# Hybrid pool, convolution and attention block: the order of stores, loads and splits around the attention stage's gate projections

## The chip, the cores and the metric

The kernel runs on one core of a Trainium2 chip. The time is the device time of one execution in microseconds (us), with all inputs and outputs in the chip's memory (HBM). Lower is better. The engines are TensorE (PE in the rows), VectorE (DVE), ScalarE (ACT), GpSimd (POOL) and SyncE (SP, which here only starts transfers; its rows read SPq).

## What is computed

One layer for x of 4096 tokens by 1024 channels, in float32. The reference, cut to what matters here:

```
h = rms_norm(x, ln_g); proj = h @ w_in
u_pool, g_pool, c_a, c_b, g_conv, q, k, v, g_attn = split_columns(proj)
y_pool = pool_mixer(u_pool, pool_w, pool_scale)
y_conv = conv_module(c_a, c_b, conv_dw, conv_b, conv_ln_g, conv_ln_b, conv_pw)
y_attn = sliding_window_attention(q, k, v, attn_sinks)   # 8 query heads, 2 kv heads, window 128, ALiBi, sinks
y = concat([y_pool * silu(g_pool), y_conv * silu(g_conv), y_attn * silu(g_attn)])
x = x + y @ w_out
return rms_norm(x, final_g)
```

## The kernel before

Tokens are worked on in eight blocks of 512 (NB = 8, n from 0), each of four subtiles of 128 (j from 0). Each float32 product is made of three passes over a rounded part (hi) and the rest (lo): hi by hi, lo by hi and hi by lo. The program has three stages, one behind the other: attention for all eight blocks (0 to about 700 us of the trace), the pool and convolution branches for all blocks, and the output projection. The weights of the output projection are prepared during the attention stage.

Every engine has its own instruction list, in the order in which the code writes it, and semaphores join them. An engine that waits holds up all that stands behind it on its list; for SyncE that is every transfer that it has yet to start. Nothing reorders the lists.

**A block n of the attention stage, on each engine.**

- TensorE (`tensor.body`): `attend(n-1, 0)`, the projections q0 to q3 (during q3 it also sums the squares of the next x, `fold_sums`), then `attend(n-1, 1)`, v, and then the gate projections g0 to g3 with the scores of subtiles 1 to 3 put inside them (scores of subtile 0 stand between v and g0), and k of the next block. `attend(n-1, 1)` multiplies the probabilities of subtiles 2 and 3 with v. It waits until they are loaded and masked, and, since it writes the bank that the sum of squares was in, also until VectorE has taken that sum (`mean`, L282).
- ScalarE (`scalar.body`): hi parts of q, hi parts of the weight sums (`combos.split_hi`, L496), the squares of the next x, `st.scale` (L294; the next x times its reciprocal root, in four parts), the exponentials of the scores, the tanh of the gates, hi parts of the next x (L333).
- VectorE (`vector.body`): lo parts of q, `make_combos` (adds two pieces of the output weights, L488, waits for ScalarE's hi part, subtracts it, L500), `mean`, `output(n-1, 1)`, `next_x(part)` (turns a scaled part of x, L301), `take_scores` (L1039, L1043), `invert`, `gate_make`, and the turning of the probabilities in squares (L1068).
- GpSimd: scales the probabilities (L840), masks them after they are loaded (`mask`, L850), and takes the reciprocal root for x (`root`, L288).

**Probabilities** are turned by way of HBM: `store_probs` (L695, four transfers) writes a subtile to `p_scratch`, and `load_probs` (L702, L704) reads it back when the store has landed. Subtiles 2 and 3 of block n-1 are loaded at the start of block n.

**Weight sums.** `Combos` makes 28 sums or pieces of the output weights, five in each of the blocks 1 to 5 and three in block 6; those of a block have the slots 0 to 4. They pass through two stages of memory in turn (`stage[s % 2]`), so VectorE or ScalarE can begin with sum s only when the store of sum s - 2 has landed (`wait_free`). `combos.store` (L506) waits for the lo part, stores 512 KB, and after some sums starts loads of the next raw weights (L461). `store_xT` (L730) stores half of the block's split x, 2048 KB.

**The last block and the change of stages.** While the last block runs, SyncE and ScalarE load weight chunks of the next stage, and SyncE loads x in parts into `x_first` (L542). TensorE begins the next stage with the projections cb0 and ca0, and then runs `attend_last`, the product of subtiles 2 and 3 of block 7 with v. VectorE's list ends the attention with `gate_last`, and all of the next stage's VectorE work stands behind that. SyncE's list for the next stage begins with small constants (L1618 to L1621, taps and per-channel vectors, fetched element by element) and the weight chunk U, and then with `turn_loads`, the last transfers of probabilities.

## Time and profile before

| | |
|---|---|
| median of 3 runs | 1484.96 us (1483.4 to 1488.67) |
| the profiled execution | 1483.98 us |
| its span, first to last instruction | 1482.0 us |
| TensorE busy | 1368.3 us, 92% |
| VectorE busy | 1174.0 us, 79% |
| ScalarE busy | 548.4 us, 37% |
| GpSimd busy | 362.0 us, 24% |
| mean granted TensorE clock | 0.972 |

The profiled execution is 0.98 us under the median, and 1.98 us of it lie outside the span. From about 700 us on, TensorE is busy nearly without a break; its idle time lies before that.

### The profile page before, as it was taken

The page shows a single profiled execution, that of the slowest core. Times are in us where ns is not written, and L with a number is a line of the kernel's source. Part 1 is how long each engine was busy: PE and PEld are TensorE (multiplying, and loading weights), DVE is VectorE, ACT ScalarE, POOL GpSimd, SP SyncE. Part 2 cuts the span into 40 slices and gives each one's busy share as a digit, 9 for nine tenths or more (in the row PEclk, how much of TensorE's full clock was granted, in tenths as well). Part 3 has the DMA queues.
Part 4 walks back from the last instruction along what each step waited for, and adds up shares of the span by engine and source line. Part 5 has one row for each costly group of instructions (what it writes and reads, how often), then busy time and mean ns, then how long its engine had stood idle before and what let it go on. Part 6 is the DMA issues. An engine that isn't in the chain of part 4 may idle for free.

```text
span 1482.0 us, 20609 instructions
## 1 busy us (share of the span) xinstructions
PE 1368.3 (92%) x7070; PEld 1118.1 (75%) x7070; DVE 1174.0 (79%) x2381; ACT 548.4 (37%) x1421; POOL 362.0 (24%) x543
## 2 busy tenths in 40 slices
PE   6997979798897979894999999999999999999998
PEld 5876767676775767683888888888888888888886
DVE  5786859577685848470989999889899998888886
ACT  5744636464554536350211212212212243333332
POOL 4222313222221313140010110101101245555552
PEclk9999999899898999997999999999999999999999
DMA  9656482946556482858430321312326656455531
GB/s 215 208 140 262 117 297 91 277 151 193 204 142 249 107 276 72 256 204 165 157 122 21 128 101 56 127 55 101 128 72 241 273 167 226 160 164 156 163 138 73
DMA packets 117547, 239.18 MB, mean 161 GB/s; under 512 B 17488, under 2 KB 75216, under 8 KB 109776
## 3 DMA queue, kind: packets, MB, share of 16 engines
q1 hardware_dynamic: 93312, 214.24, 43.6%
q10 hardware_dynamic: 24144, 23.80, 6.6%
q8 instruction: 49, 0.80, 0.2%
q14 instruction: 42, 0.34, 0.1%
HBM read 139.44 MB, written 98.57 MB: 161 GB/s over the span
## 4 chain that ended last, share of the span: by engine, by line
PE 57%; DVE 19%; DMA 12%; SPq 5%; ACT 4%; issue 3%; POOL 1%; POOLq 0%; DVEq 0%; ACTq 0%
PE wide L346 12%; PE wide L347 12%; PE wide L348 12%; DMA p_scratch<-a_rows 6%; DVE a_rows L1043 4%; DMA combo_scratch<-stage 3%; DVE m_tail L2042 3%; PE turn L1232 3%; DVE xT L339 3%; DVE wide L1039 2%; PE pair L1265 2%; DVE a_rows L1068 2%; PE pair L1266 2%; PE pair L1271 2%; ACT a_rows L899 2%
## 5 line engine op out<-in xcount | busy, mean ns | idle before, releaser
L2042 DVE SCALAR_TENSOR_TENSOR m_tail<-m_tail,m_taps 128x512 f32<-128x512 f32 x480 | 338.5, 753 | 4.6
L1271 PE MATMUL pair<-xT,w_hi 128*128 128x512 f32 x384 | 154.2, 401 | 11.0 <-DVE xT L339 10.4
L840 POOL TENSOR_SCALAR a_rows<-a_rows,a_inv 128x128 f32<-128x128 f32 x256 | 94.3, 388 | 282.0 <-DVE a_inv L1063 223.7
L1265 PE MATMUL pair<-xT,w_hi 128*128 128x512 f32 x384 | 151.6, 395 | 3.5 <-DVE w_lo L410 3.5
L1266 PE MATMUL pair<-xT,w_lo 128*128 128x512 f32 x384 | 150.5, 392 | 0.0
L1784 POOL TENSOR_TENSOR operand_sums<-m_y 128x512 f32<-128x512 f32 x75 | 102.2, 1362 | 167.6 <-PE wide L348 116.6
L346 PE MATMUL wide<-x_first,w_hi 128*128 128x512 f32 x320 | 125.6, 392 | 1.5 <-DMA x_first<-xT_scratch 1.5
L346 PE MATMUL wide<-xT,w_hi 128*128 128x512 f32 x320 | 125.2, 391 | 0.0
L348 PE MATMUL wide<-x_first,w_hi 128*128 128x512 f32 x320 | 124.6, 389 | 0.0
L347 PE MATMUL wide<-x_first,w_lo 128*128 128x512 f32 x320 | 124.6, 389 | 0.0
L348 PE MATMUL wide<-xT,w_hi 128*128 128x512 f32 x320 | 124.5, 389 | 0.0
L347 PE MATMUL wide<-xT,w_lo 128*128 128x512 f32 x320 | 124.5, 389 | 0.0
L108 POOL TENSOR_TENSOR pool_carrier<-pool_carrier 128x1 f32<-128x1 f32 x23 | 14.1, 611 | 395.3 <-DVE m_meanvar L2051 395.3
L1871 ACT ACTIVATE x_first<-operand_sums 128x512 fp32r<-128x512 f32 x80 | 50.5, 634 | 153.7 <-POOL operand_sums L1784 152.4
L1271 PEld LDWEIGHTS pair<-xT,w_hi 128*128 128x128 f32 x384 | 72.2, 188 | 39.6 <-DVE xT L339 24.3
L1265 PE MATMUL wide<-xT,w_hi 128*128 128x512 f32 x256 | 101.3, 396 | 0.0
L1271 PE MATMUL wide<-xT,w_hi 128*128 128x512 f32 x256 | 99.8, 390 | 0.0
L1266 PE MATMUL wide<-xT,w_lo 128*128 128x512 f32 x256 | 99.7, 389 | 0.0
L899 ACT ACTIVATE a_rows<-a_rows,a_negmax 128x128 f32<-128x128 f32 x256 | 99.1, 390 | 0.0
L1232 PE MATMUL turn<-a_pT,a_v 128*64 128x128 f32 x256 | 24.6, 353 | 75.1 <-DVE a_meansq L282 50.6
L1265 PEld LDWEIGHTS pair<-xT,w_hi 128*128 128x128 f32 x384 | 72.5, 189 | 17.7 <-DVE w_lo L410 3.9
L1266 PEld LDWEIGHTS pair<-xT,w_lo 128*128 128x128 f32 x384 | 72.4, 189 | 13.9
(264 smaller groups left out, 3169.5 us busy)
## 6 DMA issues: line engine op xcount, KB each, us to landing
xT_scratch<-xT SPq DMA_DIRECT2D x16, 2048.0 KB, 11.8
p_scratch<-a_rows SPq DMA_DIRECT2D x128, 128.0 KB, 2.5
x_first<-xT_scratch SPq DMA_DIRECT2D x16, 1024.0 KB, 8.3
xT<-xT_scratch SPq DMA_DIRECT2D x16, 1024.0 KB, 9.2
combo_scratch<-stage SPq DMA_DIRECT2D x28, 512.0 KB, 7.3
m_y<-y_scratch ACTq DMA_DIRECT2D x14, 1024.0 KB, 6.6
xs<-in_x_dram SPq DMA_DIRECT2D x20, 512.0 KB, 9.8
a_pT<-p_scratch SPq DMA_DIRECT2D x16, 512.0 KB, 5.0
```

What stands on the lines that cost most here:

```text
L346: nc.tensor.matmul(out, w_hi, x_hi, start=first, stop=False)
L347: nc.tensor.matmul(out, w_lo, x_hi, start=False, stop=False)
L348: return nc.tensor.matmul(out, w_hi, x_lo, start=False, stop=last)
L840: last = nc.gpsimd.tensor_scalar(probs[b][:, h], probs[b][:, h], inv[:, b, h:h + 1], 0.5, ALU.mult, ALU.mult)
L899: last = nc.scalar.activation(probs[b][:, h], probs[b][:, h], ACT.Exp, bias=negmax[:, b, h:h + 1], accum_out=rowsum[:, b, h:h + 1])
L1043: last = nc.vector.tensor_tensor_reduce(out=probs[b][:, h], in0=in_runs(score[:, h, P:]), in1=in_runs(bias[:, h]), scale=1.0, scalar=sinks ...
L1232: return nc.tensor.matmul(out, weights[keys, halves[kv]], probs_of, start=start, stop=stop)
L1265: nc.tensor.matmul(out, w.hi(c)[:, kk, cols], st.hi[:, kk, :], start=(kk == 0), stop=False)
L1266: nc.tensor.matmul(out, w.lo(c)[:, kk, cols], st.hi[:, kk, :], start=False, stop=False)
L1271: last = nc.tensor.matmul(out, w.hi(c)[:, kk, cols], st.lo[:, kk, :], start=False, stop=(kk == KT - 1))
L1784: nc.gpsimd.tensor_tensor(operand_sums[:, i, 1], y_block(q, left), y_block(q, right), SIGN[op]).then_inc(operand_sum, 1)
L2042: nc.vector.scalar_tensor_tensor(out=conv[:, i, :], in0=h[:, i, j:j + TB], scalar=taps[:, i, j:j + 1], in1=conv[:, i, :], op0=ALU.mult, op ...
```

## The change

It has four parts. (A) In blocks 1 to 6 SyncE stores the first weight sum of the block (slot 0) before `load_probs(n-1, 3)` and no longer after it and after the first `store_xT`. The second sum is stored before the first `store_xT`, the third between the two. (B) ScalarE scales parts 0 and 1 of the next x ahead of the hi parts of the weight sums 3 and 4, part 2 ahead of the first exponentials and part 3 where part 2 was; VectorE turns parts 0 and 1 before it takes the first scores, part 2 where part 1 was and part 3 where part 2 was. (C) At the end of the attention stage SyncE stores subtile 2 before it waits for the chunk GP, loads it and stores subtile 3 before the next stage's list begins, and loads subtile 3 ahead of the small constants. (D) In the last block VectorE makes the lo part of chunk GP before it inverts the sums of subtile 3.

```diff
     def turn_loads(sp):
-        load_probs(sp, NB - 1, 2)
-        store_probs(sp, NB - 1, 3)
         load_probs(sp, NB - 1, 3)
...
                 load_probs(sp, n - 1, 2)
                 store_probs(sp, n - 1, 3)
+                for s in combos.of_block(n, (0,)):
+                    combos.store(sp, s)
                 load_probs(sp, n - 1, 3)
             st.wait_loaded(sp, n + 1)
...
+            for s in combos.of_block(n, (1,)):
+                combos.store(sp, s)
             store_xT(n, 0)
-            for s in combos.of_block(n, (0, 1)):
+            for s in combos.of_block(n, (2,)):
                 combos.store(sp, s)
             store_xT(n, 1)
-            for s in combos.of_block(n, (2, 3, 4)):
+            for s in combos.of_block(n, (3, 4)):
                 combos.store(sp, s)
...
+        store_probs(sp, NB - 1, 2)
         sp.wait_ge(w.lo_done[CHUNK_GP], 1)
         load_xT(sp, x_first, x_first_loaded, xT_scratch, 0, (2,))
-        store_probs(sp, NB - 1, 2)
+        load_probs(sp, NB - 1, 2)
+        store_probs(sp, NB - 1, 3)
...
             q_hi(n, 3)
+            if not final:
+                for part in (0, 1):
+                    st.scale(act, n + 1, part)
             for s in combos.of_block(n, (3, 4)):
                 combos.split_hi(act, s)
...
             if not final:
-                for part in (0, 1):
-                    st.scale(act, n + 1, part)
                 take_v()
+                st.scale(act, n + 1, 2)
                 for kv in range(KV):
                     exps(n, 0, kv)
                 act.wait_ge(st.squared_more, st.HALF * (n + 1))
                 gate_tanh(n, 0)
-                st.scale(act, n + 1, 2)
+                st.scale(act, n + 1, 3)
...
                 gate_tanh(n, 1)
-                st.scale(act, n + 1, 3)
...
             if not final:
-                next_x(0)
+                for part in (0, 1):
+                    next_x(part)
                 for kv in range(KV):
                     take_scores(n, 0, kv)
                 invert(SUB * n, 0, 0)
-                next_x(1)
+                next_x(2)
...
                 invert(SUB * n + 1, 1, 0)
-                next_x(2)
+                next_x(3)
                 invert(SUB * n + 1, 1, 1)
                 gate_make(n, 1)
-                next_x(3)
...
                     take_scores(n, j, 1)
+                    if j == 3:
+                        w.split_lo(dve, CHUNK_GP)
                     inverts(j)
...
                 step_of_v()
-                w.split_lo(dve, CHUNK_GP)
...
         sp.wait_ge(score_taken, ATTENDED)
+        w.load(sp, CHUNK_U)
+        attention.turn_loads(sp)
...
         sp.dma_start(pw[:], conv_pw[0].rearrange("(i p) d -> p i d", p=P)).then_inc(small_loaded, 16)
-        w.load(sp, CHUNK_U)
-        attention.turn_loads(sp)
         w.load(sp, CHUNK_GC)
```

SyncE's list in block 2, before, from the end of the store of subtile 3 (`p_scratch` is where the probabilities are turned, `combo_scratch` takes the weight sums, `raw` the pieces they are made of, `xT_scratch` the split x):

```order
L695 DMA p_scratch<-a_rows 32x4x256 x3
L702 DMA a_rows<-p_scratch 128x1024 [waits pv_full,a_probs_stored1]
L704 DMA a_rows<-p_scratch 64x512 x2
L730 DMA xT_scratch<-xT 128x4096 [waits x_loaded3,x_loaded2,xT_lo_done,x_loaded1,x_loaded0]
L506 DMA combo_scratch<-stage 128x2x512 [waits combo_lo] x2
L461 DMA raw<-in_w_out_dram 128x512 x2
L730 DMA xT_scratch<-xT 128x4096 [waits xT_lo_done]
L506 DMA combo_scratch<-stage 128x2x512 [waits combo_lo] x2
```

The same place in the changed kernel:

```order
L695 DMA p_scratch<-a_rows 32x4x256 x3
L506 DMA combo_scratch<-stage 128x2x512 [waits combo_lo]
L702 DMA a_rows<-p_scratch 128x1024 [waits pv_full,a_probs_stored1]
L704 DMA a_rows<-p_scratch 64x512 x2
L506 DMA combo_scratch<-stage 128x2x512 [waits x_loaded3,x_loaded2,combo_lo,x_loaded1,x_loaded0]
L461 DMA raw<-in_w_out_dram 128x512 x2
L728 DMA xT_scratch<-xT 128x4096 [waits xT_lo_done]
L506 DMA combo_scratch<-stage 128x2x512 [waits combo_lo]
L728 DMA xT_scratch<-xT 128x4096 [waits xT_lo_done]
```

The first sum's store now stands before the load of subtile 3, the second before the first store of split x, and the third behind that store instead of behind both.

SyncE's list at the change of stages, before (`x_first` is the first x of the next stage, `m_y` receives weight chunks, `in_w_in_dram` is the input projection):

```order
L542 DMA x_first<-xT_scratch 128x2048 [waits w_lo_done7]
L695 DMA p_scratch<-a_rows 32x4x256 [waits a_probs_loaded0,a_probs_squares_turned]
L695 DMA p_scratch<-a_rows 32x4x256 x3
L1618 DMA m_taps<-in_conv_dw_dram 128x31x1 [waits score_taken,score_full]
...
L1621 DMA m_pw<-in_conv_pw_dram 128x2x256
L390 DMA m_y<-in_w_in_dram 32x8x256 x4
L702 DMA a_pT<-p_scratch 128x1024 [waits pv_full,a_probs_stored0]
L704 DMA a_pT<-p_scratch 64x512 x2
L695 DMA p_scratch<-a_rows 32x4x256 [waits a_probs_loaded1,a_probs_squares_turned]
L695 DMA p_scratch<-a_rows 32x4x256 x3
L702 DMA a_rows<-p_scratch 128x1024 [waits pv_full,a_probs_stored1]
L704 DMA a_rows<-p_scratch 64x512 x2
```

The same place in the changed kernel:

```order
L695 DMA p_scratch<-a_rows 32x4x256 [waits a_probs_loaded0,a_probs_squares_turned]
L695 DMA p_scratch<-a_rows 32x4x256 x3
L542 DMA x_first<-xT_scratch 128x2048 [waits w_lo_done7]
L702 DMA a_pT<-p_scratch 128x1024 [waits pv_full,a_probs_stored0]
L704 DMA a_pT<-p_scratch 64x512 x2
L695 DMA p_scratch<-a_rows 32x4x256 [waits a_probs_loaded1,a_probs_squares_turned]
L695 DMA p_scratch<-a_rows 32x4x256 x3
L390 DMA m_y<-in_w_in_dram 32x8x256 [waits score_taken,score_full]
L390 DMA m_y<-in_w_in_dram 32x8x256 x3
L702 DMA a_rows<-p_scratch 128x1024 [waits pv_full,a_probs_stored1]
L704 DMA a_rows<-p_scratch 64x512 x2
L1626 DMA m_taps<-in_conv_dw_dram 128x31x1
```

The nine small transfers (L1618 to L1621, now L1626 to L1629) stood ahead of the load of subtile 2 and now stand behind the load of subtile 3.

## Rows read from the trace of the kernel before

**Rows 1.** Waits from 90 to 600 us: waiter <- releaser: us, times, longest.

```profile
PE turn L1232 <- DVE a_meansq L282: 50.6, 6, 11.1
...
DVE stage_sum L488 <- DMA combo_scratch<-stage: 32.5, 6, 6.9
...
ACT stage L496 <- DMA combo_scratch<-stage: 24.5, 4, 7.4
```

**Rows 2.** Timeline of SyncE in block 2: start, us, line, transfer, count.

```profile
187.96 2.00 SPq L695 DMA_DIRECT2D p_scratch<-a_rows  x4
195.53 0.34 SPq L702 DMA_DIRECT2D a_rows<-p_scratch  x1
...
197.18 0.45 SPq L730 DMA_DIRECT2D xT_scratch<-xT  x1
197.68 2.60 SPq L506 DMA_DIRECT2D combo_scratch<-stage  x2
200.32 2.58 SPq L461 DMA_DIRECT2D raw<-in_w_out_dram  x2
```

**Rows 3.** Timeline of VectorE in block 2; in brackets idle before and releaser.

```profile
199.91 1.39 DVE L1088 SCALAR_TENSOR_TENSOR a_q<-wide,a_q 64x512 fp32r<-64x512 f32 x2
206.32 0.69 DVE L488 TENSOR_TENSOR stage_sum<-raw 128x512 f32<-128x512 f32 x1 [5.02 <-DMA combo_scratch<-stage]
...
208.43 0.17 DVE L282 TENSOR_SCALAR a_meansq<-turn 128x16 f32<-128x16 f32 x1
...
218.40 0.69 DVE L500 TENSOR_TENSOR stage<-raw,stage 128x512 fp32r<-128x512 f32 x1 [6.25 <-ACT stage L496]
...
238.26 1.25 DVE L301 STREAM_TRANSPOSE xs<-xs 128x1024 f32<-128x1024 f32 x1 [0.92 <-ACT xs L294]
```

**Rows 4.** Timeline of ScalarE, then of GpSimd, in block 2.

```profile
217.73 0.63 ACT L496 ACTIVATE stage<-raw 128x512 fp32r<-128x512 f32 x1 [6.32 <-DMA combo_scratch<-stage]
218.27 3.30 ACT L294 ACTIVATE xs<-xs,a_rstd 128x256 f32<-128x256 f32 x8
...
200.09 1.29 POOL L850 TENSOR_TENSOR a_rows<-a_rows 128x512 f32<-128x512 f32 x1 [4.06 <-DMA a_rows<-p_scratch]
208.69 2.91 POOL L288 TENSOR_TENSOR a_rstd<-a_meansq,a_power 128x16 f32<-128x16 f32 x1 [7.31 <-DVE a_meansq L282]
```

**Rows 5.** Timeline of TensorE: first quarter of an attend, at 175 and 208 us.

```profile
175.41 1.09 PE L1232 MATMUL turn<-a_pT,a_v 128*64 128x128 f32 x16
...
208.66 1.97 PE L1232 MATMUL turn<-a_pT,a_v 128*64 128x128 f32 x16 [7.63 <-DVE a_meansq L282]
```

**Rows 6.** Windows: stretch, length, busy by engine, granted clock, DMA share, GB/s.

```profile
94.99:593.94 498.95, 434.14 (x2634) 346.81 (x2630) 349.13 (x999) 253.77 (x820) 119.04 (x222) 0.95 0.60 188
176.94:259.11 82.17, 72.21 (x443) 57.65 (x440) 58.34 (x169) 42.38 (x137) 19.89 (x37) 0.96 0.62 196
201.00:208.60 7.60, 0.03 (x1) 0.00 (x0) 1.85 (x4) 1.50 (x3) 0.38 (x1) 0.78 0.96 358
```

**Rows 7.** Timeline of SyncE at the change of stages.

```profile
666.30 2.45 SPq L695 DMA_DIRECT2D p_scratch<-a_rows  x4
...
681.03 0.40 SPq L702 DMA_DIRECT2D a_pT<-p_scratch  x1
...
682.70 1.96 SPq L695 DMA_DIRECT2D p_scratch<-a_rows  x4
690.53 0.34 SPq L702 DMA_DIRECT2D a_rows<-p_scratch  x1
```

**Rows 8.** Timeline of GpSimd and TensorE at the change of stages.

```profile
696.45 1.26 POOL L850 TENSOR_TENSOR a_rows<-a_rows 128x512 f32<-128x512 f32 x1 [5.66 <-DMA a_rows<-p_scratch]
...
666.51 0.62 PE L1232 MATMUL turn<-a_rows,a_pT 64*64 64x128 f32 x16
671.60 0.50 PE L346 MATMUL wide<-x_first,w_hi 128*128 128x512 f32 x1 [1.52 <-DMA x_first<-xT_scratch]
...
697.86 1.97 PE L1232 MATMUL turn<-a_pT,a_v 128*64 128x128 f32 x16 [17.80 <-POOL a_rows L850]
```

## The prediction

> **What bounds the kernel now.** I read the waits first, then the timelines of one block. Over the six blocks 1 to 6 of the attention stage TensorE stands still 50.6 us in six waits before `attend`, put down to VectorE's `mean` [rows 1]. In the same stretch VectorE waits 32.5 us and ScalarE 24.5 us for stores of weight sums to land. The reader is to see one chain in them, and the timelines of block 2 show it. SyncE issues the store of subtile 3 at 187.96, then stands until 195.53 for it to land before it can issue the load, and only after that, and after 2048 KB of split x, starts the store of the first weight sum, at 197.68 [rows 2]. VectorE is done with the lo part of q2 at 201.30 and then waits 5.02 us, to 206.32, because the third sum needs the memory of the first. So `mean` runs at 208.43 [rows 3] and TensorE, idle for 7.63 us, resumes at 208.66 [rows 5]. The first sum landed 8.6 us after its issue, right behind the 2048 KB. Within the wait the granted clock falls (0.78 over the idle stretch [rows 6]; between the levels 2.4 and 1.2 GHz that is full clock for some 4.3 of 7.6 us), and the first quarter of the attend takes 1.97 us, against 1.09 where TensorE came to it without a pause [rows 5].
>
> The fifth sum repeats this: it needs the third one's memory. The third was stored at 208.4, behind the second store of split x, and ScalarE's wait for it, 6.32 us, ends at 217.73 [rows 4]. VectorE's lo part follows at 218.40, and everything of the second half of the block stands behind it on VectorE's list. Block 2 takes 82.17 us and the six blocks 498.95 [rows 6].
>
> The second place is the change of stages. TensorE waits 17.80 us for GpSimd's mask of subtile 3 [rows 8]. Its load was issued at 690.53, its store at 682.70, and the load of subtile 2 before them at 681.03. The stretch from 668.75, the end of the store of subtile 2, to 681.03 is SyncE issuing nine small transfers and one weight chunk [rows 7]. After that TensorE has no gap of this kind.
>
> **Part A, the first sum's store.** No work is added; one 512 KB store is issued at 190.0 (187.96 + 2.00) instead of 197.68. Its lo part has been ready since before, so SyncE waits for nothing new. Even with the same 8.6 us it lands by 198.6, before VectorE wants the memory at 201.30. From there the sum's add, hi and lo take 0.69, 0.7 and 0.69 us, so `mean` runs at 203.4, 5.0 us earlier. TensorE's wait shrinks from 7.6 to 2.6 us, and its clock should stay full, since the fall came later than that.
>
> What is late next is the fifth sum. The third is stored at about 203.4: the second sum's store and two loads of raw weights are issued by 202.9 [rows 2], then comes the first store of split x, then the third sum. It again stands behind 2048 KB, so I take 8.0 us (row: 8.6, with a load of probabilities ahead as well that has by then been served; bounds 6.5 and 9.5). It lands at 211.4. ScalarE's hi part takes 0.63 us, VectorE's lo part starts at 212.1 instead of 218.40: 6.3 us earlier.
>
> Who waits for the store that is now ahead? The load of subtile 3. It is issued at the same 195.53 but has up to 512 KB more before it on the same queue, at the 358 GB/s of this stretch [rows 6] 1.5 us. GpSimd's mask then ends at about 202.9 instead of 201.38 [rows 4], still before 203.4. The bounds are 0 and 2 us; 2 would hold TensorE, not VectorE, which by my estimate is the later of the two by 1.4 us or more. The first store of split x is issued at 203 instead of 197.2; its memory is rewritten only near the end of the block, so that costs nothing.
>
> The Trainium skill, page "DMA: Bandwidth & Descriptors", section "Queues, rings and completion order", speaks against this edit: a queue's descriptors are taken in order on each engine, and the completion count is written only after all earlier writes of that engine, across queues. By that rule the load of subtile 3 cannot complete before the moved store, whatever its own size. The sum by it is the one above with 1.5 us on the mask, so nothing is lost in block 2, and up to 1.5 us where the mask comes last.
>
> **Part B, scaled x earlier.** The eight scalings take 3.30 us. They ran at 218.27, behind the hi part that waited for the store [rows 4]. Now they start when GpSimd's root is done: 203.6 + 2.91 = 206.5, ending at 209.8, inside ScalarE's wait. VectorE now turns two parts instead of one before the first scores, 1.25 us more there, and one fewer behind them. The last part's wait of 0.92 us [rows 3] goes too, because it is scaled one step earlier. So the first scores come 6.3 - 1.25 = 5.1 us earlier, and the end of the block 5.1 + 1.25 + 0.92 = 7.2 us earlier. Bound of the gain of part B alone: 0 to 2.2 us a block. In block 0 there are no sums; the turn ahead of the scores costs about 1.7 us there (half of the 3.30) and is given back behind. I take 0.
>
> **Sum of A and B.** Block 2 goes from 82.17 to 75.0 us. TensorE is busy 72.2 us in it [rows 6], of which nearly 2 us are the slow clock, so 75 is above its floor of about 70.5. The other blocks have the same work and their own lengths only from the same waits (the longest wait of the six is 11.1 us [rows 1]), so I take 75.0 for blocks 1 to 5, and 73.0 for block 6, which has no fourth and fifth sum. 5 x 75.0 + 73.0 = 448; 498.95 - 448 = 51 us gained. With the third sum landing in 9.5 instead of 8.0 us and 1.5 us more lost elsewhere it is 33; with 6.5 us TensorE becomes the limit after another 1.4 us a block, and it is 59.
>
> **Parts C and D.** D puts 2.3 us of VectorE work between the last scores and the inversion of their sums, in time in which ScalarE takes the exponentials; the subtile is turned about when it was. Priced 0, bound 1.5 us either way. For C, subtile 2 is stored before the chunk GP is waited for. Its load needs the memory that `attend(7, 0)` reads until 667.1 [rows 8]; it takes 1.67 us to issue (681.03 to 682.70 [rows 7]). The store of subtile 3 thus starts at 668.8 instead of 682.70, 13.9 us earlier. From that start to the end of its mask it took 15.0 us before (682.70 to 697.71): with the same delays the mask ends at 683.8. Before, one weight chunk and the load of subtile 2 lay unfinished ahead of the store; now the chunk lies behind it, ahead of the load. I take 2.8 us off: 681.0. TensorE gets there earlier too: x_first's part 2 is issued sooner, the 1.52 us wait [rows 8] goes, and its two projections end at 678.5. It waits 2.6 instead of 17.80 us and starts the attend 16.8 us earlier. At full clock the attend itself is shorter, by 0.9 us in its first quarter (1.97 against 1.09 [rows 5, 8]) and, by estimate, 2.6 us over all four. Together 19 us, bounds 12 (transfers as slow as before and a fallen clock) and 21. From there on TensorE is busy without a gap and the shift is kept to the end.
>
> **The sum.** 51 + 19 = 70 us off the profiled execution's 1483.98: 1414. The median is 0.98 above that execution, which makes 1415; I say **1414**, since the blocks 3 to 5 waited longer before than block 2.
>
> **Rivals.**
>
> 1. The second half gives part back: the third sum, behind 2048 KB, lands in 11 to 12 us, or x of the next block, whose loads share the queue with the moved store, comes later and holds VectorE before the second q. Then a block takes 78.5 to 79 us. For it: the DMA engines are busy 0.96 in this stretch [rows 6]. Against: the bytes are the same and a gap of 3 us opens. 5 x 78.7 + 76.5 = 470, 29 us gained; with 19: 1436.
> 2. The small constants come last. They are now issued from about 675 for 10 us and land near 688, while VectorE, after `attend_last` at about 684, wants the taps near 687. Against: TensorE needs what hangs on them only one projection later. If it bites, the change of stages gives 10: 1424.
> 3. Slower: the load of subtile 3 gets stuck behind the moved store in each block. It decides from the point where the mask ends after 208.5, that is, where the load lands more than 7 us later than now. If both took the place of the slowest rows of their kind, some 4 us a block would be lost after the gain is gone, 6 x 4 = 24, and with 19 - 0 kept at the change of stages the time is 1490. Only a wait of that size in every block does it, and 512 KB are 1.5 us.
> 4. The edit does not free the chain: the third sum waits for something else than the first one's store, such as raw weights or ScalarE. Then only the change of stages is won: 1465. Against: the wait of 5.02 us names the store [rows 3].
>
> **Chances.** Forecast 0.60 (its own range 1404 to 1428), rival 1 0.22, rival 2 0.10, rival 3 0.03, rival 4 0.05. The range must leave out no more than 0.2: 1402 to 1440 takes in the bounds of the sum and the rivals 1 and 2. Within 0.3%, 4.5 us, is about what a measurement of this kernel can tell from no change; only some of rival 3 lies there. Faster 0.96, same 0.02, slower 0.02.
>
> **What would show it.** In the profile after: first sum's store right behind the store of subtile 3; VectorE's wait for `combo_scratch` before `mean` gone; TensorE's six waits at `attend` 1 to 3 us each with the clock near 1.0; block length 73 to 76 us; the last mask at 680 to 684. Wrong would be: blocks of 78 us or more with ScalarE or VectorE waiting for the third sum (rival 1), VectorE idle before the taps after `gate_last` (rival 2), or GpSimd's mask as the last release of the attend with waits above 4 us (rival 3).

## The result, and the profile after

| | before | changed |
|---|---|---|
| median | 1484.83 us (1483.4 to 1488.67) | 1420.58 us (1418.57 to 1422.36) |
| ratio, 95% interval | | 0.9563 (0.9539 to 0.9587) |
| span of the profiled execution | 1482.0 us | 1417.2 us |
| six blocks, 1 to 6 | 498.95 us | 449.70 us |
| end of `attend(7, 0)` to end of `attend_last` | 36.3 us | 20.95 us |
| from there to the end | 778.6 us | 778.5 us |

The change saves 64 us. The spans differ by 64.8: 49.3 of them lie in the six blocks, 15.4 in the change of stages, and the rest of the program is only shifted. A block is taken, as in [rows 6], from the start of the third turning of squares (L1068, now L1073) to the next such start. The six are now 75.61, 76.90, 74.75, 72.20, 75.43 and 74.81 us.

The waits of the changed kernel from 85 to 560 us (waiter, releaser: us, times, longest), to be read against [rows 1]:

```profile
PE turn L1238 <- DVE a_meansq L282: 11.6, 5, 3.6
...
PE turn L1238 <- POOL a_rows L854: 2.7, 1, 2.7
...
DVE stage_sum L488 <- DMA combo_scratch<-stage: 17.9, 3, 7.0
...
ACT stage L496 <- DMA combo_scratch<-stage: 1.4, 1, 1.4
```

TensorE's 50.6 us before the second attend are 14.3. One of the six waits before, the longest (11.1 us, in block 5), did not go back to the landing of the first sum's store. There VectorE's idle time ahead of `mean` was for raw weights:

```profile
458.25 0.69 DVE L488 TENSOR_TENSOR stage_sum<-raw 128x512 f32<-128x512 f32 x1 [8.64 <-DMA raw<-in_w_out_dram]
```

Their load stands right behind the store of the first sum on SyncE's list, so the same order held it back. Block 2, SyncE, the stretch of [rows 2] (start, us, line, transfer, count):

```profile
181.20 1.99 SPq L695 DMA_DIRECT2D p_scratch<-a_rows  x4
...
183.24 0.47 SPq L506 DMA_DIRECT2D combo_scratch<-stage  x1
188.96 0.34 SPq L702 DMA_DIRECT2D a_rows<-p_scratch  x1
...
194.88 0.46 SPq L728 DMA_DIRECT2D xT_scratch<-xT  x1
197.49 0.38 SPq L506 DMA_DIRECT2D combo_scratch<-stage  x1
```

The first sum leaves 5.7 us ahead of the load of subtile 3, not 2.2 us behind it. VectorE in the same block, to be read against [rows 3] (in brackets idle before and releaser):

```profile
194.41 1.66 DVE L488 TENSOR_TENSOR stage_sum<-raw 128x512 f32<-128x512 f32 x1
196.77 0.69 DVE L500 TENSOR_TENSOR stage<-stage_sum,stage 128x512 fp32r<-128x512 f32 x1 [0.70 <-ACT stage L496]
197.49 0.17 DVE L282 TENSOR_SCALAR a_meansq<-turn 128x16 f32<-128x16 f32 x1
...
206.56 0.69 DVE L500 TENSOR_TENSOR stage<-raw,stage 128x512 fp32r<-128x512 f32 x1 [1.33 <-ACT stage L496]
```

The third sum's add comes without a wait, and the lo part of the fifth sum runs 36.2 us behind the block's start, before 41.5. TensorE, the second attend in three of the six blocks, and the windows of the six blocks (length, busy by engine, granted clock, DMA share, GB/s), against [rows 5] and [rows 6]:

```profile
120.60 1.09 PE L1238 MATMUL turn<-a_pT,a_v 128*64 128x128 f32 x16 [1.50 <-DVE a_meansq L282]
197.72 1.97 PE L1238 MATMUL turn<-a_pT,a_v 128*64 128x128 f32 x16 [3.60 <-DVE a_meansq L282]
273.89 1.09 PE L1238 MATMUL turn<-a_pT,a_v 128*64 128x128 f32 x16 [2.75 <-POOL a_rows L854]
...
94.80:544.50 449.70, 427.52 (x2633) 341.98 (x2630) 349.64 (x998) 253.12 (x820) 119.30 (x222) 0.98 0.67 209
```

The other three waited 1.65, 2.92 and 1.96 us. Of a block's 75 us TensorE is now busy 71.3. In block 7, which the change leaves as it was, TensorE waits 6.77 us for the mask at the same place in both kernels:

```profile
574.75 1.98 PE L1238 MATMUL turn<-a_pT,a_v 128*64 128x128 f32 x16 [6.77 <-POOL a_rows L854]
```

The change of stages, SyncE, then GpSimd, TensorE and VectorE, against [rows 7] and [rows 8]:

```profile
619.43 2.30 SPq L695 DMA_DIRECT2D p_scratch<-a_rows  x4
621.83 2.33 SPq L390 DMA_DIRECT2D m_y<-in_w_in_dram  x4
624.88 0.34 SPq L702 DMA_DIRECT2D a_rows<-p_scratch  x1
...
626.39 0.59 SPq L1626 DMA_DIRECT2D m_taps<-in_conv_dw_dram  x1
627.02 5.52 SPq L1628 DMA_DIRECT2D m_conv_bias<-in_conv_b_dram  x1
632.59 0.48 SPq L1628 DMA_DIRECT2D m_ln_gain<-in_conv_ln_g_dram  x1
...
632.92 1.26 POOL L854 TENSOR_TENSOR a_rows<-a_rows 128x512 f32<-128x512 f32 x1 [9.27 <-DMA a_rows<-p_scratch]
...
634.33 1.97 PE L1238 MATMUL turn<-a_pT,a_v 128*64 128x128 f32 x16 [5.47 <-POOL a_rows L854]
...
642.43 0.20 DVE L2008 TENSOR_SCALAR m_taps<-m_taps 128x62 f32<-128x62 f32 x1
```

TensorE waits 5.47 us instead of 17.80. The load of subtile 3 is issued at 624.88 and its mask starts at 632.92, 8.0 us later; before it was 5.9 [rows 7, 8]. VectorE finds the taps there without a wait.

### The profile page after: what moved, and what is told of

It reads as the page before. It is cut to its first block, busy times and chain, and to the rows that moved or that the text cites. A ratio compares the mean times of both kernels' runs of the same rounds, so it can differ in the third digit from the quotient of the medians.

```text
span 1417.2 us, 20609 instructions
## 1 busy us (share of the span) xinstructions
PE 1359.6 (96%) x7070; PEld 1111.9 (78%) x7070; DVE 1174.1 (83%) x2381; ACT 547.0 (39%) x1421; POOL 360.8 (25%) x543
## 4 chain that ended last, share of the span: by engine, by line
PE 58%; DVE 21%; DMA 9%; ACT 5%; issue 3%; SPq 3%; POOL 1%; ACTq 0%; POOLq 0%; DVEq 0%
PE wide L346 12%; PE wide L348 12%; PE wide L347 12%; DMA xs<-in_x_dram 5%; DVE a_rows L1048 4%; DVE m_tail L2048 3%; DVE xT L339 3%; PE pair L1271 2%; DVE wide L1044 2%; PE pair L1272 2%; PE pair L1277 2%; PE turn L1238 2%; PE turn L347 2%; PE pair L347 2%; PE pair L348 2%
## 5 line engine op out<-in xcount | busy, mean ns | idle before, releaser
L108 POOL TENSOR_TENSOR pool_carrier<-pool_carrier 128x1 f32<-128x1 f32 x23 | 14.1, 612 | 394.1 <-DVE m_meanvar L2057 394.1
L1277 PEld LDWEIGHTS pair<-xT,w_hi 128*128 128x128 f32 x384 | 72.2, 188 | 33.9 <-DVE xT L339 18.4
L1048 DVE CUSTOM_DVE_ANT_0 a_rows<-wide,a_bias,a_sinks 128x128 f32<-128x128 f32 x256 | 74.6, 347 | 2.3
```

Of the source, the lines that this page charges most:

```text
L1048: last = nc.vector.tensor_tensor_reduce(out=probs[b][:, h], in0=in_runs(score[:, h, P:]), in1=in_runs(bias[:, h]), scale=1.0, scalar=sinks ...
L1277: last = nc.tensor.matmul(out, w.hi(c)[:, kk, cols], st.lo[:, kk, :], start=False, stop=(kk == KT - 1))
```

## The experiments

"Blocks" is the length of blocks 1 to 6 in the trace, "stretch" goes from the end of `attend(7, 0)` to the end of `attend_last`, "last wait" is TensorE's wait ahead of the latter. All in us. The ratio is to the kernel before on the same chip, with its 95% interval.

| kernel | median | ratio | blocks | stretch | last wait |
|---|---|---|---|---|---|
| before | 1484.83 | | 498.95 | 36.3 | 17.80 |
| changed | 1420.58 | 0.9563 (0.9539 to 0.9587) | 449.70 | 20.95 | 5.47 |
| changed, again | 1421.04 | 0.9563 (0.9550 to 0.9576) | 449.66 | 22.2 | 5.50 |
| before + A | 1441.48 | 0.9701 (0.9674 to 0.9728) | 456.91 | 35.2 | 16.68 |
| changed without B | 1430.50 | 0.9619 (0.9598 to 0.9640) | 459.62 | 21.7 | 6.18 |
| before + C | 1473.59 | 0.9912 (0.9885 to 0.9940) | 501.61 | 25.35 | 7.87 |
| changed without D | 1420.73 | 0.9562 (0.9539 to 0.9586) | 447.19 | 24.96 | 7.59 |
| load 3 ahead of U | 1415.37 | 0.9513 (0.9491 to 0.9536) | 449.70 | 16.9 | 2.75 |
| same, constants last | 1422.82 | 0.9574 (0.9560 to 0.9589) | 448.23 | 19.9 | 3.21 |
| third sum ahead | 1415.76 | 0.9530 (0.9501 to 0.9560) | 444.93 | 23.2 | 7.37 |
| before + mean ahead | 1468.34 | 0.9885 (0.9861 to 0.9909) | 484.39 | 34.2 | 16.95 |
| load 3 and mean ahead | 1414.10 | 0.9521 (0.9497 to 0.9546) | 446.22 | 16.8 | 2.73 |
| all three ahead | 1404.07 | 0.9447 (0.9434 to 0.9461) | 438.73 | 16.4 | 2.32 |
| split x ahead of load 3 | 1441.63 | 0.9709 (0.9693 to 0.9725) | 469.76 | 21.5 | 5.81 |

Where the code of the blocks is the same, their sum differs by up to 2.7 us from profile to profile (449.70, 449.66, 449.70, 448.23 and 447.19; 498.95 and 501.61). The stretch differs by 2.3 (five profiles whose code is the same there gave 20.95, 21.5, 21.7, 22.2 and 23.2). So a few us in a single trace decide nothing. The rows were measured on several chips, on which the kernel before had medians of 1484.5 to 1486.7, so between rows the ratios compare better than the medians. The spread of the profiles was looked for with the changed kernel itself, run once more:

> The changed kernel itself once more, beside the version with the three edits, so that the two are compared on one chip, and to see how far the stretch from attend(7, 0) to the end of attend_last differs from profile to profile: it was 20.95 us here, and 21.7 and 23.2 in two runs whose code is the same there, against 24.96 and 25.35 without part D. Expected: 1418 to 1423 us, stretch 20.5 to 23.5. If it comes out at 24 or more, the 4 us that I put down to part D are nothing but spread.

1421.04 us and a stretch of 22.2, as expected.

**The parts one by one.** Part A alone, on the kernel before:

```diff
                 store_probs(sp, n - 1, 3)
+                for s in combos.of_block(n, (0,)):
+                    combos.store(sp, s)
                 load_probs(sp, n - 1, 3)
...
+            for s in combos.of_block(n, (1,)):
+                combos.store(sp, s)
             store_xT(n, 0)
-            for s in combos.of_block(n, (0, 1)):
+            for s in combos.of_block(n, (2,)):
...
-            for s in combos.of_block(n, (2, 3, 4)):
+            for s in combos.of_block(n, (3, 4)):
```

> The kernel before with part A alone: the stores of the weight sums in their new places on SyncE, the scalings of x and the last block as they were. Theory (one chain: the store of the first sum frees the third, the third frees the fifth): the mean runs some 4.4 us earlier in block 2 than before, the six waits before attend are 1.5 to 4 us each, and a block is 76 to 77.5 us, since the eight scalings, 3.3 us, stand behind a hi part that comes earlier. Six blocks 458 us (455 to 466), against 449.7 in the changed kernel and 498.95 before; the 17.80 us wait at the last mask stays. Time about 1441 us (1436 to 1449). Rival (the gain of the blocks is mostly the early scaling): blocks of 79 us or more, time 1455 or more.

1441.5 us, blocks 456.91, the longest wait before `attend` 3.6, as the theory said. Part A carries 42 of the 49 us of the blocks. It moves three stores at once, and no run moves the first one alone, so what the second and third contribute is not shown. Part B undone in the changed kernel:

```diff
             q_hi(n, 3)
-            if not final:
-                for part in (0, 1):
-                    st.scale(act, n + 1, part)
             for s in combos.of_block(n, (3, 4)):
...
             if not final:
+                for part in (0, 1):
+                    st.scale(act, n + 1, part)
                 take_v()
...
```

(and parts 2 and 3, and the four turns on VectorE, back to where they were).

> The changed kernel with part B undone: scalings and turns of the next x where they stood before, everything else kept. Theory: a block is 1 to 2 us longer than in the changed kernel (74.9 on average), so six blocks 456 to 462, and the time 1420.6 + 9 = 1429 us (1424 to 1434). Rival 1: the scalings fit anyway into ScalarE's waits, and ScalarE's hi part of the fourth sum, which waits 4.7 us behind them in the changed kernel, is now free: no difference, 1418 to 1423. Rival 2: the early scaling carries the gain: 1440 or more.

1430.5 us, blocks 459.62: part B is worth 7.2 us by the first run (456.91 - 449.70) and 9.9 by this one, 1.2 to 1.7 us a block. Part C alone, on the kernel before:

```diff
+        store_probs(sp, NB - 1, 2)
         sp.wait_ge(w.lo_done[CHUNK_GP], 1)
         load_xT(sp, x_first, x_first_loaded, xT_scratch, 0, (2,))
-        store_probs(sp, NB - 1, 2)
+        load_probs(sp, NB - 1, 2)
+        store_probs(sp, NB - 1, 3)
...
+        w.load(sp, CHUNK_U)
+        attention.turn_loads(sp)
...
```

> The kernel before with part C alone: subtile 2 stored ahead of the wait for the chunk GP, chunk U and the load of subtile 3 ahead of the small constants; part D, the subtraction for GP, stays behind the step of v. Theory: the change of stages, from the end of attend(7, 0) to the end of attend_last, goes from 36.3 to 21 us as in the changed kernel, the rest stays: 1484.8 - 15.4 = 1469.4 us (1467 to 1472). Rival (part D has a share, since with GP's lo part later part 2 of x_first is issued later and the two projections behind it): the stretch is 22.5 us or more, TensorE waits at the projections, time 1471 to 1474.

1473.6 us and a stretch of 25.35: both in the rival's ranges. The stretch is 11 us shorter than before, in the changed kernel 15.4. Part D seemed to have a share, so it was undone alone in the changed kernel:

```diff
-                    if j == 3:
-                        w.split_lo(dve, CHUNK_GP)
...
                 step_of_v()
+                w.split_lo(dve, CHUNK_GP)
```

> The changed kernel with part D alone undone: the subtraction for the chunk GP stands behind the step of v again. In the kernel with part C alone the stretch from the end of attend(7, 0) to the end of attend_last came out at 25.35 us, not at the 20.95 of the changed kernel. Theory (part D has the share that I priced at 0): GP's lo part is late, so part 2 of x_first is issued some 5 us later, right ahead of the load of subtile 2 and the store of subtile 3, and these land later; the stretch is 24 to 26 us, the last mask waits for its load 7 us or more, the time is 3 to 4.5 us more, about 1424. Rival (my price of 0; the 25.35 of the other run came from what its blocks left behind): stretch 20 to 22 us, time 1419 to 1422.

The order in time is as the theory said. Without part D x's part 2 goes out right ahead of the load of subtile 2, and TensorE waits 7.59 us. SyncE and GpSimd of this kernel:

```profile
614.00 0.35 SPq L542 DMA_DIRECT2D x_first<-xT_scratch  x1
615.38 0.34 SPq L702 DMA_DIRECT2D a_pT<-p_scratch  x1
...
633.40 1.26 POOL L854 TENSOR_TENSOR a_rows<-a_rows 128x512 f32<-128x512 f32 x1 [8.87 <-DMA a_rows<-p_scratch]
```

In the changed kernel part 2 went out 5.1 us ahead of that load. But the median does not differ (1420.73 against 1420.58 and 1421.04). The two stretches without part D are 2 to 4 us longer than the five with it. In this profile the blocks are 2.5 us shorter, which hides most of it; that is no more than their spread. Whether part D is worth anything stays open.

**What holds a block.** The kernel before with `mean` moved, and nothing else:

```diff
-                if t == 3 and not final:
+                if t == 3 and first:
                     st.mean(dve, n + 1)
                 make_q_lo(n, t)
+                if t == 2 and not first and not final:
+                    st.mean(dve, n + 1)
                 make_combos(n, (t,) if t < 3 else (3, 4))
```

> The kernel before with one line moved: the mean on VectorE ahead of the third weight sum; all stores where they were. It frees TensorE's attend from the wait for the first sum's landing, but not VectorE, which still waits 5.02 us for the third sum's memory and ScalarE 6.32 us for the fifth's. Theory 1 (my sum: a block ends when VectorE's list does, whose second half stands behind the fifth sum's landing): the waits before attend shrink from 50.6 us to under 15, but a block loses no more than 3 us: 1465 to 1480 us. Theory 2 (TensorE's waits set the blocks; VectorE's are cover): 5 to 7 us a block, as much as the change brought: 1440 to 1455 us.

1468.3 us. The waits for `mean` are gone, and 8.1 us remain for the mask. VectorE and TensorE in block 2 of this kernel:

```profile
201.88 0.17 DVE L282 TENSOR_SCALAR a_meansq<-turn 128x16 f32<-128x16 f32 x1
208.98 0.69 DVE L488 TENSOR_TENSOR stage_sum<-raw 128x512 f32<-128x512 f32 x1 [6.92 <-DMA combo_scratch<-stage]
...
218.62 0.69 DVE L500 TENSOR_TENSOR stage<-raw,stage 128x512 fp32r<-128x512 f32 x1 [4.03 <-ACT stage L496]
...
202.42 1.09 PE L1234 MATMUL turn<-a_pT,a_v 128*64 128x128 f32 x16 [1.31 <-POOL a_rows L850]
```

TensorE starts the attend 6.2 us earlier than in [rows 5]. VectorE waits longer for the first sum's landing, 6.92 us, and its last lo part runs at 218.62, against 218.40 [rows 3]. TensorE then waits for VectorE and ScalarE later in the blocks: 11.6 us in nine waits before scores, where it was 3.8, and 11.6 in five for ScalarE's tanh. Blocks 1 to 5 go down by only 1.2 us each on average; block 6, which has no fourth and fifth sum, by 8.6 (82.65 to 74.01). So blocks 1 to 5 were held by the chain of sums on VectorE's list, and TensorE could not use the time that it no longer waited for `mean`. Block 6 was held by `mean` itself. That is what my sum assumed for blocks 1 to 5, and here it is shown.

**What holds it now.** The changed kernel with the third sum stored ahead of the first 2048 KB:

```diff
-            store_xT(n, 0)
             for s in combos.of_block(n, (2,)):
                 combos.store(sp, s)
+            store_xT(n, 0)
```

> The changed kernel with the third weight sum stored ahead of the first store of split x instead of behind its 2048 KB. My forecast made the landing of the third sum the next limit of a block (8.0 us, bounds 6.5 and 9.5). Theory A (as forecast): it lands in some 4 us, VectorE's waits for it (three of 4.6 to 7.0 us, 17.9 us in all) go, the second half of blocks 1, 3 and 5 starts earlier, 2 to 4 us a block: 1408 to 1415 us. Theory B (in the changed kernel TensorE has no wait behind the attend, so it is the limit there and VectorE's waits cost nothing): VectorE's waits go and its wait for TensorE's scores grows by the same; block lengths within 0.5 us of the changed kernel's on average, 1418 to 1423 us. I hold B the likelier.

VectorE's three waits of 17.9 us fall to 1.11, 1.68 and 1.27. Block 1 gets 3.1 us shorter, the others between 1.2 shorter and 0.5 longer. Only block 1 moved as theory A said, and the other five are close to theory B. The median, 4.8 us lower, lies between the two ranges, and the intervals of the two ratios overlap, so the gain itself is not clear of the noise. And the `mean` ahead, with the load of subtile 3:

```diff
+        attention.turn_loads(sp)
         w.load(sp, CHUNK_U)
-        attention.turn_loads(sp)
```

(with the edit of `mean` above).

> A version that may beat both: the changed kernel with the load of subtile 3 ahead of chunk U, as in the run before, and the mean on VectorE ahead of the third weight sum instead of behind its lo part (in block 2 of the changed kernel the fold that it reads ends at 189.93, but mean runs at 197.49). Theory (TensorE waits for mean only because of its place in VectorE's list): mean runs at about 194.4, the attend then waits for GpSimd's mask, which ends at 195.52, so each of the six waits shrinks to 0.5 to 1.5 us and the clock stays full in the attend: some 2 us a block, 1.5 to 3, together 10 to 16 us: 1400 to 1406 us, from 1415.4. Rival (VectorE's list sets the second half of a block, whatever TensorE does): the waits before the attend shrink, but come back before the scores or behind them; less than 4 us in all, 1411 to 1416 us.

1414.1 us, in the rival's range, and by the ratios no faster than without the `mean` edit (0.9521 against 0.9513). `mean` runs at 194.28 in block 2 and the waits before `attend` fall to 8.6 us in six. But TensorE's waits before scores rise from 1.6 to 5.9 us, and VectorE's waits for the third sum stay. The longest of TensorE's stands in block 2:

```profile
215.80 0.74 PE L1302 MATMUL wide<-a_k_lo,a_q 64*128 64x256 f32 x8 [3.51 <-DVE a_rowmax L1048]
```

Block 2 is 76.90 us long, as in the changed kernel. All three together:

> The best version by the runs so far: the changed kernel with the load of subtile 3 ahead of chunk U (-5.2 us alone), the third sum's store ahead of the first store of split x (-4.8 us alone) and the mean ahead of the third sum (-1.3 us on top of the first of them). Theory 1 (the mean's gain came back before the scores because VectorE was held by the fifth sum; with the third sum stored early both engines are free): a block is 72.5 us on average, six blocks 435, 1420.6 - 5 - 14 = 1402 us (1398 to 1406). Theory 2 (TensorE's work is the floor from here on, the gains only add up): six blocks 441 to 444, 1406 to 1411 us.

1404.07 us, where the changed kernel took 1421.04 on the same chip: **this version beats both** the kernel before and the changed one. The three edits together gain 17 us. By medians of different chips they were 5.2, 4.8 and 1.3 by themselves, 11.3 in all, and the intervals of the ratios are too wide to show that the whole is more than the sum. The time is in the range of theory 1, the blocks, 438.73, between the two theories. What the traces show beyond a sum lies in block 2: 76.90 us in the changed kernel and with `mean` ahead, 75.68 with the third sum ahead, 72.41 with both, where the wait of 3.51 us is gone. Five profiles with the code of the changed kernel there have 75.7 to 76.9. TensorE's waits from 85 to 560 us, and the windows of the six blocks:

```profile
PE turn L1240 <- POOL a_rows L854: 9.0, 6, 2.8
PE pair L1279 <- DVE xT L339: 4.6, 19, 0.7
PE turn L276 <- DVE a_sumsq L248: 1.7, 4, 0.6
...
94.73:533.46 438.73, 424.13 (x2634) 340.11 (x2630) 348.47 (x998) 252.50 (x820) 120.15 (x222) 0.99 0.69 214
```

What TensorE still waits for in a block is the mask, 1.5 us, and some 1 us for the parts of the next x; its own work takes 70.7.

**The landing of the last load.** The exchange of chunk U and the load of subtile 3 alone:

> The changed kernel with one exchange: the load of subtile 3 ahead of the four parts of chunk U in SyncE's list. In the changed kernel that load is issued at 624.88 and lands only at 632.9, 8 us later; TensorE waits 5.47 us and its clock falls. Theory (U's 1 MB, issued 3 us ahead on the same queue, delays it): the load lands in 5 to 6 us, 3 us earlier, TensorE waits 2.5 us or less with its first quarter at 1.09, and the time is 3 to 5 us less, 1416 to 1418 us. U then lands later and may hold TensorE's turn of U: if so, some of it is given back. Rival (the small constants behind it delay it): the load lands at 632 to 633 all the same and the time stays within 1 us of 1420.6.

SyncE, GpSimd, TensorE and VectorE of this kernel:

```profile
623.88 0.34 SPq L702 DMA_DIRECT2D a_rows<-p_scratch  x1
...
625.39 2.06 SPq L390 DMA_DIRECT2D m_y<-in_w_in_dram  x4
...
629.79 1.26 POOL L854 TENSOR_TENSOR a_rows<-a_rows 128x512 f32<-128x512 f32 x1 [6.47 <-DMA a_rows<-p_scratch]
...
631.20 1.09 PE L1238 MATMUL turn<-a_pT,a_v 128*64 128x128 f32 x16 [2.75 <-POOL a_rows L854]
...
643.75 0.20 DVE L2008 TENSOR_SCALAR m_taps<-m_taps 128x62 f32<-128x62 f32 x1 [3.78 <-DMA m_pw<-in_conv_pw_dram]
```

5.9 us from issue to mask, the wait 2.75, the clock full: U's 1 MB was the cause. The other profiles agree. In the seven with U issued shortly ahead of this load it takes 8.0 to 10.5 us from issue to mask, in the four with U behind it 5.4 to 6.3. The stretch is 4.1 us shorter. Some 1.4 us come back behind it: the small constants land 2 us later, and VectorE now waits 3.78 us for them. Their turn to go last:

```diff
         attention.turn_loads(sp)
         w.load(sp, CHUNK_U)
+        w.load(sp, CHUNK_GC)
         with nc.allow_non_contiguous_dma(reason="per-channel constants, once"):
...
-        w.load(sp, CHUNK_GC)
```

> The changed kernel with the load of subtile 3 ahead of chunk U, as in the run of that name (1415.4 us, load issued to landed 5.9 us, TensorE waits 2.75 us), and with the small constants and the 1x1 weights behind chunk GC as well. Theory: the 8.0 us of the changed kernel were U's 1 MB alone, the constants' small packets take nothing from the load: it lands in 5.5 to 6 us again, the last wait is 2.3 to 3.2 us, and the constants, now issued some 2 us later, still land before VectorE's first tap: 1414 to 1417 us. Rival 1 (they still slow the load): it lands in 4.9 us or less, TensorE waits 1.7 or less, 1413 to 1414.5. Rival 2 (my old one, that the constants come last): VectorE waits for the taps, TensorE behind it, 1418 us or more.

The load takes 6.3 us, no less than with the constants close behind it, so they were no burden to it. But my second rival, that the constants come last, is now true. SyncE, VectorE and TensorE:

```profile
629.84 11.36 SPq L1629 DMA_DIRECT2D m_conv_bias<-in_conv_b_dram  x1
...
650.31 0.20 DVE L2008 TENSOR_SCALAR m_taps<-m_taps 128x62 f32<-128x62 f32 x1 [7.59 <-DMA m_pw<-in_conv_pw_dram]
...
654.32 3.78 PE L2337 MATMUL turn<-m_pool_lhs,m_sums 128*128 128x128 f32 x16 [5.04 <-DVE m_sums L2112]
```

1422.8 us, 7.4 more than with the constants in front of GC.

**The third rival made strong.** In blocks 1 to 6 of the changed kernel the first store of split x, 2048 KB, goes out ahead of the load of subtile 3 (block 7 has its own list, which the edit does not touch):

```diff
                     combos.store(sp, s)
+                store_xT(n, 0)
                 load_probs(sp, n - 1, 3)
...
-            store_xT(n, 0)
+            if n == 0:
+                store_xT(n, 0)
```

> My third rival, made four times as strong: the changed kernel with the first store of split x, 2048 KB, ahead of the load of subtile 3 in every block 1 to 7, behind the first sum's store. In the changed kernel the load takes 4.65 to 5.3 us from issue to its mask, with 512 KB put ahead of it, against 4.56 to 4.76 before. Theory (bytes ahead cost the load only what has not been served when it is issued; the 2048 KB go out some 5 us before it, in the time in which SyncE waits for the store of subtile 3, and at 358 GB/s need 5.7 us): the load lands 0 to 2 us later, the mask still ends before or about with the mean, the third sum finds its queue free as with its store put ahead: 1415 to 1422 us. Rival (all of the 2048 KB stand before the load, as by the Trainium skill, DMA: Bandwidth & Descriptors, Queues, rings and completion order, its completion follows theirs): masks 4 to 6 us later, TensorE waits 4 to 6 us for GpSimd and not for the mean: 1430 to 1445 us.

1441.6 us, inside the rival's range. Block 2, SyncE, GpSimd and TensorE, then the landing of the load and, last, of that store in this kernel (windows 180 to 205 us and 186.40 to 186.95; KB, us from issue to landing):

```profile
186.43 0.54 SPq L728 DMA_DIRECT2D xT_scratch<-xT  x1
192.16 0.33 SPq L702 DMA_DIRECT2D a_rows<-p_scratch  x1
...
201.09 1.26 POOL L856 TENSOR_TENSOR a_rows<-a_rows 128x512 f32<-128x512 f32 x1 [8.67 <-DMA a_rows<-p_scratch]
...
202.49 1.97 PE L1240 MATMUL turn<-a_pT,a_v 128*64 128x128 f32 x16 [5.90 <-POOL a_rows L856]
...
a_rows<-p_scratch SPq DMA_DIRECT2D x1, 512.0 KB, 7.0
...
xT_scratch<-xT SPq DMA_DIRECT2D x1, 2048.0 KB, 12.0
```

The landing of the load in the changed kernel (176 to 202 us):

```profile
a_rows<-p_scratch SPq DMA_DIRECT2D x1, 512.0 KB, 4.1
```

From issue to mask it is 8.6 to 10.0 us in blocks 1 to 6, against 4.7 to 5.3 in the changed kernel. The store had been under way for 5.7 us when the load was issued, and I had taken it to be served by then, at 358 GB/s. But it landed 12.0 us after its issue (11.3 to 12.3 in the six blocks), and the load behind it. TensorE waits 33.9 us in six for the mask, and the clock falls.

The Trainium skill, page "DMA: Bandwidth & Descriptors", section "Queues, rings and completion order", says that each DMA engine consumes a ring's descriptors in order and that the completion count is written only after all its earlier writes. This trace agrees: the load lands after the store, at 199.2 (192.16 + 7.0) against 198.4 (186.43 + 12.0). The order of these two landings is all that it shows of the rule, and not every pair of transfers on this queue keeps it: in block 2 of the kernel before, the last piece of the load of subtile 2 (64x512), issued at 187.27, landed at 194.5, and the first piece of the store behind it, issued at 187.96, at 193.9. So the words "whatever its own size" in my prediction say more than the traces bear out.

## Why the prediction was right, point by point

- **The sum.** 70 us were forecast and 64 measured; 1414 against 1420.6, in the range of 1402 to 1440 and in the forecast's own range. The blocks gave 49.3 of the 51 us. That this came so close is in part luck: I had worked out block 2 alone, at 75.0, and taken the same for the others. Against the forecast the six are 0.6, 1.9, -0.3, -2.8, 0.4 and 1.8 us longer, and block 4, which came out shorter than anything I had worked out, pays for blocks 2 and 6.
- **Part A.** `mean` runs 27.1 us behind the block's start, before 31.5: 4.4 us earlier, not 5.0. The third sum's add took 1.66 us, where [rows 3] has 0.69; why is not shown. The lo part of the fifth sum runs 36.2 us behind the start, where I had 35.2.
- **The clock** was to stay full. It did in blocks 1, 3 and 4, where the attend takes 3.00 us. In block 2 it had fallen before the attend began (first quarter 1.97 us after a wait of 3.60, the attend 5.59 us), and in blocks 5 and 6 it fell within the attend (4.61 and 4.56 us). So the sentence "its clock should stay full" held for half of the blocks. The three slow attends cost 2.6, 1.6 and 1.6 us. Block 6 is 74.81 us here and 72.7 to 73.0 in four other profiles of the same block code, in which its attend takes 3.00.
- **The third sum's landing**, 8.0 us with bounds 6.5 and 9.5: 8.4 us in block 2 (issue at 197.49, ScalarE's hi part at 205.90); in blocks 1, 3 and 5, 9.3, 8.7 and 6.2. The size was right, but for the last, just under its bound. Its weight was not quite: I made it the next limit of every block, and storing the third sum early moved one block by 3.1 us. In the others TensorE was already busy for all but 2.2 to 4.3 us, most of them the wait ahead of the attend.
- **The load of subtile 3** behind 512 KB: up to 1.5 us. From issue to mask it was 4.67 us before and 4.90 now on average, at most 5.30: 0.2 us. In block 3 the mask is what TensorE waits for last. The price of rival 3 was sound for this size, and the run with 2048 KB shows where it stops being so.
- **Part B**, 0 to 2.2 us a block: 1.2 to 1.7.
- **Part C is the term that was mis-sized**: 19 forecast, 15.4 measured (14.1 in the second profile, still above its bound of 12). Its first steps came as worked out: the store of subtile 3 starts 1.7 us behind the end of `attend(7, 0)`, and TensorE is ready 11.1 us behind it (forecast 11.4). What failed is the sentence "now the chunk lies behind it, ahead of the load. I take 2.8 us off". The store did land sooner (5.5 us from its issue to the load's, against 7.8), but the chunk cost the load 2.1 us (8.0 against 5.9 from issue to mask; up to 10.5 in the other profiles). From store to mask's end it is 14.75 us instead of 15.0, not 12.2. With the wait of 5.47 us, where I had 2.6, the clock fell as well: the attend takes 4.35 us instead of 3.00. The run with the load ahead of U gives both back, and its stretch of 16.9 is 19.4 us under the one before.
- **Part D**, 0 with a bound of 1.5: the medians agree with 0, the traces don't quite; open.
- **Rivals.** Rival 1 (blocks of 78 us) did not come: no block exceeded 76.9. Rival 2 did not bite in the changed kernel, but with the load ahead of U it does, by 1.4 us. Rival 4 fell with the result and the run of part A alone, although the raw weights that it named were what VectorE waited for in block 5 before. Of the signs that I had named, the block length (73 to 76 us) missed block 2 with 76.9 and block 4 with 72.2, and one of the six waits, 3.60 us, was above 3. The last mask came at the late end of its range, 16.4 us behind the end of `attend(7, 0)`, where 680 to 684 is 12.9 to 16.9.
- **Kept to the end**: 778.5 us behind `attend_last` against 778.6, as forecast.

## What to carry to other kernels

When an engine waits for an instruction that stands behind another engine's wait, look for what holds up the head of that list. Moving the waited-for instruction alone freed TensorE and gave 16 us, more than half of it in the one block without a fourth and fifth sum; moving the stores that free the memory gave 45. When a block has two holders of nearly the same length, an edit against one of them can leave it as long as it was: block 2 lost 0 and 1.2 us by one edit each and 4.5 by both. So judge such edits together. Ahead of an urgent load on a queue, count what has not landed when it is issued, by landing times from the trace (12 us for the 2 MB store here), and not what seems unserved at the peak rate.

## What the hardware showed that I had not expected

- SyncE itself can be held by a small transfer. Issuing `m_conv_bias`, 128 single elements, kept it for 5.5 us in the changed kernel and 11.4 us with 2 MB of weights issued shortly ahead, where its like right behind it (`m_ln_gain`) took 0.43 to 1.0 us in all profiles. So it is not the vector's own size. What stands right ahead of it is `m_taps`, 128 x 31 single elements, and in every profile SyncE came free 1.1 to 2.5 us before `m_taps` landed (632.5 against 634.1 in the changed kernel, 641.2 against 642.3 with 2 MB ahead). Why is not shown. While these transfers ran alone (633 to 639 us) the DMA engines were busy 0.50 at 17 GB/s.
- The length of a pause alone does not say whether the clock falls. After a wait of 2.92 us the first quarter of an attend took 1.25 us in one profile and 1.98 in another; after 2.02 us it took 1.37, and after 4.02 us 1.09. A first quarter of 1.09 us does not mean that the attend stays fast either: in block 6 of the changed kernel the second one took 1.73, and the whole 4.56 instead of 3.00.
